# A two-block transformer kernel on one core: small vectors from one load, another order at the start, another split of the layer norms

## The chip, the cores and the metric

The kernel runs on one core of a Trainium2 chip. The metric is device time in microseconds (us), lower is better. Engines are called by their short names: PE (TensorE, matmul), DVE (VectorE), ACT (ScalarE), POOL (GpSimd), SP (the queue that issues the large loads).

## The reference, cut to what matters

256 tokens of width 1024 pass through two blocks. All is float32.

```
# first block: two layers
shift, scale, gate = split(silu(c) @ mod_w[i] + mod_b[i], 3)
h = rms_norm(x, norm_g[i]) * (1 + scale) + shift
x = x + gate * mixer_i(h)              # i = 0 retention, i = 1 forgetting attention
x = rms_norm(x, final_g)
# second block: two layers
x = layer_norm(ALPHA * x + mix_i(x), ln_mix_g[i], ln_mix_b[i])   # gated conv of 31 taps; short conv
x = layer_norm(ALPHA * x + ffn_i(x), ln_ffn_g[i], ln_ffn_b[i])   # dense SwiGLU of 2816; 8 experts, top 2
# layer_norm(z) = (z - mean) * rsqrt(var + 1e-5) * g + b
```

## The kernel before, in words

Each engine has its own program, written out by hand; semaphores tie them. An engine runs its instructions strictly in the order of its program, so that an instruction behind one that waits is late as well.

**Weights.** SP loads weights in chunks of 2 MB into a ring of three slots (`load`, L616), in the order of `LOADS`. A chunk before the experts is 512 columns of a first matrix, or 4 blocks of 128 rows of a second one. Before the chunks of weights, and between them in the retention, come halves of the three parts of `mod_w` (SCALE, SHIFT, GATE), two to a part. A slot is loaded anew when DVE has used what lay in it. A chunk is split into high and low parts for exact products, half by half (a half is a "unit"; four unit buffers): ACT copies the high part (`highs_until`, L1134), DVE subtracts (`lows_until`, L1461). ACT may write a unit buffer only when PE is done with the unit that lay there four units before (`released`, L557). Each product on PE is three matmuls (`product`, L690: lines 692 to 694).

**The start.** ACT issues the small loads: the vector `c` (8 rows), the identity and the rope exponents, the positions, eight loads of vectors, one vector to a partition, 43 rows of 1024 in all (the 31 taps of the convolution are one of them, L1105), and the rest of the constants. PE turns `c` and the vectors into columns (L797, L801) and DVE copies the columns to `vec` (L1596). DVE computes the rope angles (`angles`), multiplies and adds the rows of the SCALE and SHIFT halves of `mod_w` with silu(c) (`modulation`, L1529 and L1531; eight instructions a part), normalises x between the first and the second half (`normalise`, L1567), and PE sums over partitions (`mod_sum`, L792). SP loads x behind the first half of SCALE. When both sums are there, ACT makes the affine step on the turned x (`affine`, L1168) in four groups, DVE splits each group, and then ACT and DVE split the first two chunks of weights (`highs_until(1)`, L1187, and `lows_until(1)`, L1605). The first product waits for the whole first chunk.

**Second matrices.** `out_product` (L743) computes 2 token halves x 2 column halves in four PSUM banks. It goes through the blocks of rows with all four banks, but the last blocks (the "tail": the last 4, for `ffn_down` with its 22 blocks the last 2) first for token half 0 and then for token half 1, so that the banks of half 0 are full earlier. When a unit of the tail has been used for token half 1, it is released.

**The residual and the norms.** After `ret_out` and `fox_out`, `gated_residual` (L1587, L1589) takes bank after bank. After `conf_out`, `ffn_down` and `sc_out`, `layer_norm` (L1849) does, on DVE and for one token half after the other: z = ALPHA * x + bank and `bn_stats` for each column half (L1857, L1860), `bn_aggr`, a request to POOL for the power of -0.5 (`ask_root`, L1485; POOL's line is L1424), (z - mean) * g (L1867), a wait for the root, and x = z * root + b (L1869). Then PE transposes x (L704), ACT copies the high part out of the banks (`high_in`, L1177; for the router L1350), DVE takes the low part (`low_in`), and the next first matrix starts. Before `layer_norm` in DVE's program stands a `lows_until` for the first chunk of the next matrix; the second chunk's stands behind `low_in`.

**The experts.** Eight experts, each with 21 chunks of weights, follow in loops, and a last layer norm.

## Time and profile before

| | us |
|---|---|
| median of 3 runs (lowest to highest) | 1935.29 (1934.23 to 1935.48) |
| the profiled execution, its own time | 1935.74 |
| its span, first to last instruction | 1934.0 |
| PE busy in it | 1803.0 (93%) |
| DVE busy | 1471.2 (76%) |
| ACT busy | 1062.2 (55%) |
| POOL busy | 34.1 (2%) |

The profiled execution's time and its span differ by what lies before the first and after the last instruction. PE's busy share is an average over stages: it has gaps at the start, around the norms and where the router runs. What an edit is worth is read at the place where it stands, in the chain of waits and in the timeline of the engines there. A row of the timeline gives the start, the duration, the engine, the line, the operation and its tile, how many it merges, and in square brackets how long the engine had been idle and what released it. Busy times of neighbouring instructions on one engine overlap a little; the distance of their starts is what one costs in a row of them.

### The profile page before, as it was taken

The numbers are of one execution on the slowest core, as the hardware profiler recorded it, in microseconds if no ns is written. First come the engines' busy times: TensorE is split into PE (matmuls) and PEld (weight loads), VectorE is DVE, ScalarE is ACT, GpSimd is POOL, SyncE is SP. The second block draws the span as 40 slices with busy tenths as digits, with TensorE's granted clock in tenths as the row PEclk, the third lists the DMA queues.
The fourth block names the chain that finished last, engine by engine and source line by source line (L and its number), as shares of the span: only waits on it lengthen the run. The fifth ranks groups of instructions, "written<-read, shape, count | busy, mean of one in ns | idle before, by whom it ended". The sixth has DMA issues, their size and how long they took to land.

```text
span 1934.0 us, 23674 instructions
## 1 busy us (share of the span) xinstructions
PE 1803.0 (93%) x9475; PEld 1547.6 (80%) x9475; DVE 1471.2 (76%) x1339; ACT 1062.2 (55%) x912; POOL 34.1 (2%) x34
## 2 busy tenths in 40 slices
PE   2899889988988999897999999999999999999995
PEld 2888678868978998796788887888878888888884
DVE  5686856485976554576788888889888898888895
ACT  1334234553843333232767777767677677777772
POOL 0000002000000000000000000000000000000000
PEclk9999889999999999897999999999999999999998
DMA  9588354405304547454699999999999999999992
GB/s 339 189 301 318 114 214 162 174 14 188 138 1 137 190 153 261 142 186 152 245 339 351 368 366 337 342 354 377 350 342 346 365 361 346 354 361 371 355 380 96
DMA packets 209604, 506.75 MB, mean 262 GB/s; under 512 B 6549, under 2 KB 8877, under 8 KB 209496
## 3 DMA queue, kind: packets, MB, share of 16 engines
q1 hardware_dynamic: 204832, 498.09, 70.6%
q10 hardware_dynamic: 4488, 6.58, 1.0%
q8 instruction: 81, 1.33, 0.3%
q0 software_dynamic: 176, 0.53, 0.1%
q14 instruction: 27, 0.22, 0.0%
HBM read 504.13 MB, written 1.05 MB: 261 GB/s over the span
## 4 chain that ended last, share of the span: by engine, by line
PE 86%; DVE 8%; ACT 2%; issue 2%; DMA 1%; POOL 1%; ACTq 0%; POOLq 0%; DVEq 0%
PE psum L692 27%; PE psum L694 26%; PE psum L693 26%; DVE R L1800 2%; PE psum L1013 2%; PE psum L1041 1%; DVE units L1457 1%; DMA ring<-in_mod_w 1%; POOL root_out L1424 1%; PE psum L1082 1%; DVE stats L1860 1%; DMA R<-in_positions 0%; DVE R L1531 0%; DVE x L1869 0%; PE psum L704 0%
## 5 line engine op out<-in xcount | busy, mean ns | idle before, releaser
L1457 DVE TENSOR_TENSOR units<-ring,units 128x2048 fp32r<-128x2048 f32 x451 | 1012.5, 2278 | 241.0 <-ACT units L1148 167.9
L1365 ACT CAST units<-ring 128x2048 fp32r<-128x2048 f32 x332 | 629.7, 1914 | 244.5 <-PE psum L694 145.9
L692 PE MATMUL psum<-units,xr 128*128 128x512 f32 x1120 | 444.1, 397 | 8.0 <-issue 4.5
L694 PE MATMUL psum<-units,xr 128*128 128x512 f32 x1120 | 438.4, 391 | 0.0
L693 PE MATMUL psum<-units,xr 128*128 128x512 f32 x1120 | 438.1, 391 | 0.0
L1148 ACT CAST units<-ring 128x2048 fp32r<-128x2048 f32 (+1 forms) x119 | 218.4, 1879 | 223.2 <-PE psum L694 187.2
L692 PE MATMUL psum<-units,H 128*128 128x512 f32 x696 | 274.6, 395 | 2.2 <-DVE H L1457 2.2
L694 PE MATMUL psum<-units,H 128*128 128x512 f32 x696 | 272.4, 391 | 0.0
L693 PE MATMUL psum<-units,H 128*128 128x512 f32 x696 | 272.4, 391 | 0.0
L692 PE MATMUL psum<-xr,units 128*128 128x256 f32 x864 | 247.1, 286 | 12.7 <-DVE units L1457 11.4
L692 PEld LDWEIGHTS psum<-units,xr 128*128 128x128 f32 x1120 | 211.6, 189 | 52.7 <-issue 7.6
L694 PEld LDWEIGHTS psum<-units,xr 128*128 128x128 f32 x1120 | 211.6, 189 | 45.0
L693 PEld LDWEIGHTS psum<-units,xr 128*128 128x128 f32 x1120 | 211.8, 189 | 43.6 <-issue 0.7
L693 PE MATMUL psum<-xr,units 128*128 128x256 f32 x864 | 246.4, 285 | 0.0
L694 PE MATMUL psum<-xr,units 128*128 128x256 f32 x864 | 246.3, 285 | 0.0
L692 PEld LDWEIGHTS psum<-xr,units 128*128 128x128 f32 x864 | 168.0, 194 | 13.8 <-DVE units L1457 11.4
L693 PEld LDWEIGHTS psum<-xr,units 128*128 128x128 f32 x864 | 168.0, 194 | 0.0
L694 PEld LDWEIGHTS psum<-xr,units 128*128 128x128 f32 x864 | 167.8, 194 | 0.0
L692 PEld LDWEIGHTS psum<-units,H 128*128 128x128 f32 x696 | 131.7, 189 | 30.1 <-issue 1.9
L694 PEld LDWEIGHTS psum<-units,H 128*128 128x128 f32 x696 | 131.6, 189 | 27.7
L693 PEld LDWEIGHTS psum<-units,H 128*128 128x128 f32 x696 | 131.8, 189 | 27.0
L2014 DVE TENSOR_TENSOR R<-R,psum 128x512 f32<-128x512 f32 x56 | 38.5, 687 | 46.1 <-PE psum L694 45.8
(242 smaller groups left out, 1210.0 us busy)
## 6 DMA issues: line engine op xcount, KB each, us to landing
ring<-in_moe_w_gate SPq DMA_DIRECT2D x56, 2048.0 KB, 9.5
ring<-in_moe_w_up SPq DMA_DIRECT2D x56, 2048.0 KB, 9.4
ring<-in_moe_w_down SPq DMA_DIRECT2D x56, 2048.0 KB, 9.6
ring<-in_mod_w SPq DMA_DIRECT2D x12, 2048.0 KB, 9.9
ring<-in_ret_w_in SPq DMA_DIRECT2D x11, 2048.0 KB, 10.1
ring<-in_fox_w_in SPq DMA_DIRECT2D x8, 2048.0 KB, 8.5
ring<-in_sc_w_in SPq DMA_DIRECT2D x6, 2048.0 KB, 7.9
ring<-in_ffn_w_gate SPq DMA_DIRECT2D x5, 2048.0 KB, 8.0
```

The costliest lines, as they stand in the source:

```text
L692: mm(dst, left[0], right[0], start=first, stop=False)
L693: mm(dst, left[0], right[1], start=False, stop=False)
L694: return mm(dst, left[1], right[0], start=False, stop=last)
L1013: last = mm(psum[:, k // 4, (k % 4) * P:(k % 4 + 1) * P], x[:, tt, k * P:(k + 1) * P], e_sel[q][:, tt, :], start=(tt == 0), stop=(tt == NT ...
L1041: last = nc.tensor.transpose(b[:, j * P:(j + 1) * P], e_ht[:, (q * PAIRS + c) % 2, j * P:(j + 1) * P], ident)
L1082: last = mm(psum[:, 2 * tt + c, :], e_selT[:, tt * P:(tt + 1) * P], e_y[part][:, c * 512:(c + 1) * 512], start=(part == 0), stop=(part == 1))
L1148: nc.scalar.copy(dst[0], src).then_inc(unit_high, 3 - len(parts))
L1365: nc.scalar.copy(*expert_unit_parts(q, j, half, 0)).then_inc(unit_high, 1)
L1424: nc.gpsimd.tensor_tensor(root_out[:, n % 2, 0:w], root_in[:, n % 2, 0:w], neg_half[:, 0:w], ALU.pow).then_inc(root_ready, 1)
L1457: return v.tensor_tensor(dst, src, high.bitcast(F32), ALU.subtract)
L1800: ins = v.scalar_tensor_tensor(conv[:, i, :], u_pad[:, i, k:k + T], vec[:, i, V_DW + k:V_DW + k + 1], conv[:, i, :], ALU.mult, ALU.add)
L2014: v.tensor_tensor(e_ht[:, (q * PAIRS + c) % 2, :], e_s[:, (q * PAIRS + c) % 2, :], psum[:, 4 + (q * 2 * PAIRS + 2 * c + 1) % 4, :], ALU.mu ...
```

## The change

**Small vectors.** The host lays all vectors out feature-major, as one array of 128 partitions x 8 x 49 (three rows more than before: the shifts of three layer norms), and one load on ACT's queue, behind the constants, brings them straight to `vec`. The vector `c` comes as eight columns of the first piece of the constants. The nine small loads, PE's transposes of them and DVE's copy are gone.

**The start.** SP issues the second half of SCALE before x. DVE does both halves of SCALE before `normalise`. The first chunk of weights is split before the affine step: on ACT `highs_until(0)` stands ahead of `affine`, on DVE `lows_until(0)` stands between the second half of SHIFT and `take_sum(0, SHIFT)`. PE sums SCALE before it transposes x.

**Second matrices.** The tail goes through its blocks for token half 0, then for token half 1 and column half 0, then for token half 1 and column half 1. For `ffn_down` it is the last 6 blocks instead of the last 2. A unit of the tail is released in the third pass.

**Three layer norms** (`mix0`, `ffn0`, `mix1`). DVE does the statistics as before and (z - mean) * g in two halves of 512 columns; ACT multiplies them by the root, in place; PE transposes z, without the shift. The shift is a bias per feature, on ACT when it takes the high part (an instruction of 256 columns for each of eight blocks, before one of 512 for two blocks), and on DVE when it takes the low part (the same). Behind that DVE adds the shift to z for the x of the next residual (`shift_rows`). The last layer norm stays as it is.

```diff
...
                 sp.dma_start(dst, src).then_inc(slot_filled[at % RING], 16)
             load(0)
+            load(1)
             sp.dma_start(x[:, :, :], t["x"][0].rearrange("(t p) d -> p t d", p=P)).then_inc(x_loaded, 16)
-            load(1)
-            load(2)
-            for at in range(3, LOADED):
+            for at in range(2, LOADED):
                 load(at)
             def expert(e, q, more, number):
...
                 banks = [take_bank(OUT_BANKS[name], i) for i in range(4)]
-                def block(k, tt, w):
-                    for c in range(2):
+                def block(k, tt, w, cs=(0, 1)):
+                    for c in cs:
                         last = product(banks[2 * tt + c], [a[:, k, tt * P:(tt + 1) * P] for a in src],
                                        [a[:, k % 2, c * 512:(c + 1) * 512] for a in w], k == 0, k == blocks - 1)
                         if k == blocks - 1:
                 def weights(k):
                     return unit(CHUNK_AT[name, k // ROWS], k % ROWS // 2, lambda a: as_rows(a, 2))
-                tail = blocks % ROWS or ROWS
+                tail = blocks % ROWS + ROWS if blocks % ROWS else ROWS
                 for k in range(blocks - tail):
                     if k % 2 == 0:
                         ready(k // 2)
                         last.then_inc(weights_used, 1)
                 w = {}
-                for tt in range(NT):
+                for tt, cs in ((0, (0, 1)), (1, (0,)), (1, (1,))):
                     for k in range(blocks - tail, blocks):
                         if tt == 0 and k % 2 == 0:
                             ready(k // 2)
                             w[k // 2] = weights(k)
-                        last = block(k, tt, w[k // 2])
-                        if tt == NT - 1 and k % 2 == 1 and k < blocks - 1:
+                        last = block(k, tt, w[k // 2], cs)
+                        if cs == (1,) and k % 2 == 1 and k < blocks - 1:
                             last.then_inc(weights_used, 1)
+            def transpose_scaled(name, z, n):
+                banks = [take_bank(name, g) for g in range(4)]
+                for tt in range(NT):
+                    for g in range(4):
+                        if g % 2 == 0:
+                            pe.wait_ge(scaled, 4 * n + 2 * tt + g // 2 + 1)
+                        for j in range(2):
+                            last = nc.tensor.transpose(banks[g][:, j * T + tt * P:j * T + (tt + 1) * P],
+                                                       z[:, tt, (2 * g + j) * P:(2 * g + j + 1) * P], ident)
+                        if tt == NT - 1:
+                            last.then_inc(bank_filled, 1)
...
-            pe.wait_ge(ident_loaded, 16)
-            pe.wait_ge(c_loaded, 16)
-            nc.tensor.transpose(take_bank("c_cols", 0)[:, 0:KB], c_rows, ident[0:KB, 0:KB]).then_inc(bank_filled, 1)
-            pe.wait_ge(vec_loaded, 8 * 16)
-            b = take_bank("vecs", 0)
-            for k in range(KB):
-                last = nc.tensor.transpose(b[:, k * NVEC:(k + 1) * NVEC], vec_rows[:, k * P:(k + 1) * P],
-                                           ident[0:NVEC, 0:NVEC])
-            last.then_inc(bank_filled, 1)
-            transpose_in("x0T", xn, lambda tt: pe.wait_ge(xn_ready, tt + 1))
             pe.wait_ge(const_loaded, 16)
             mod_sum(0, SCALE)
+            pe.wait_ge(ident_loaded, 16)
+            transpose_in("x0T", xn, lambda tt: pe.wait_ge(xn_ready, tt + 1))
             mod_sum(0, SHIFT)
...
             out_product("conf_out", conf_uT, KB, lambda g: pe.wait_ge(conf_low, g + 1))
-            transpose_in("x3T", x, lambda tt: pe.wait_ge(x_ready, NT + tt + 1))
+            transpose_scaled("x3T", z_mix0, 0)
...
         @block.scalar
         def _(act):
-            act.dma_start(c_rows, t["c"].rearrange("o (k p) -> (o k) p", p=P)).then_inc(c_loaded, 16)
-            act.dma_start(const[:, 0:C_INV + 1], t["const"][:, 0:C_INV + 1]).then_inc(ident_loaded, 16)
+            act.dma_start(const[:, 0:C_TRI], t["const"][:, 0:C_TRI]).then_inc(ident_loaded, 16)
             act.dma_start(pos_i, t["positions"][0:1, :].to_broadcast([P, T])).then_inc(pos_loaded, 16)
-            for lo, src in ((V_NORM, t["norm_g"]), (V_CB, t["conf_b_dw_2"]),
-                            (V_CG, t["conf_ln_g_2"]), (V_CBETA, t["conf_ln_b_2"]),
-                            (V_SC, t["sc_w_conv_2"][0]), (V_DW, t["conf_w_dw_2"][0])):
-                act.dma_start(vec_rows[lo:lo + src.shape[0], :], src).then_inc(vec_loaded, 16)
-            for layer in range(2):
-                act.dma_start(vec_rows[V_MB + 2 * layer:V_MB + 2 * layer + 2, :],
-                              t["mod_b"][layer:layer + 1, 0:2 * D].rearrange("o (j d) -> (o j) d", d=D)).then_inc(vec_loaded, 16)
             act.dma_start(const[:, C_TRI:C_END], t["const"][:, C_TRI:C_END]).then_inc(const_loaded, 16)
+            act.dma_start(vec[:, :, :].rearrange("p k n -> p (k n)"), t["vecs"]).then_inc(vec_loaded, 16)
             def load_small():
                 act.dma_start(wf[:, :, :], cols(w_fox, 4 * D, FH)).then_inc(small_loaded, 16)
             def wait_mod_columns(i):
                 act.wait_ge(mod_columns, i + 1)
+            def scale_rows(name, z, n):
+                for tt in range(NT):
+                    i = ROOTS.index(f"{name}_{tt}")
+                    act.wait_ge(root_ready, i + 1)
+                    for half in range(2):
+                        part = z[:, tt, half * 512:(half + 1) * 512]
+                        act.wait_ge(centred, 4 * n + 2 * tt + half + 1)
+                        nc.scalar.activation(part, part, ACT.Identity, scale=root_out[:, i % 2, 0:1]).then_inc(scaled, 1)
+            def shifted_high(name, dst, n):
+                for g in range(4):
+                    b = pairs(bank(name, g))
+                    for j in range(2):
+                        k = 2 * g + j
+                        last = nc.scalar.activation(dst[:, k, :], b[:, j, :], ACT.Identity, bias=vec[:, k, V_LB + n:V_LB + n + 1])
+                    last.then_inc(bank_high, 1)
             def high_in(name, dst, n=4):
                 for g in range(n):
                     nc.scalar.copy(dst[:, 2 * g:2 * g + 2, :], pairs(bank(name, g))).then_inc(bank_high, 1)
-            nc.scalar.activation(c_act[:, :], bank("c_cols", 0)[:, 0:KB], ACT.Silu).then_inc(emptied["A"], 1)
+            act.wait_ge(ident_loaded, 16)
+            nc.scalar.activation(c_act[:, :], const[:, C_C:C_C + KB], ACT.Silu).then_inc(c_ready, 1)
             act.wait_ge(x_loaded, 16)
             square_rows(xn)
             act.wait_ge(ang_ready, 1)
             nc.scalar.activation(cos, ang[:, 4, :], ACT.Sin)
             nc.scalar.activation(sin, ang[:, 3, :], ACT.Sin).then_inc(trig_ready, 1)
+            highs_until(0)
...
-            act.wait_ge(x_ready, NT * 2)
-            high_in("x3T", xr[:, 0])
+            scale_rows("mix0", z_mix0, 0)
...
+            scale_rows("ffn0", z_ffn0, 1)
+            shifted_high("x4T", xr[:, 0], 1)
+            highs_until(CHUNK_AT["ffn_down", 5] + 2)
             act.wait_ge(x_ready, NT * 3)
             load_rows(t["ln_mix_g_2"][1:2, :], t["ln_mix_b_2"][1:2, :])
-            high_in("x4T", xr[:, 0])
...
             highs_until(CHUNK_AT["sc_out", 1] + 1)
-            act.wait_ge(x_ready, NT * 4)
+            scale_rows("mix1", z_mix1, 2)
             for g in range(4):
-                nc.scalar.copy(x5T[:, 2 * g:2 * g + 2, :], pairs(bank("x5T", g))).then_inc(emptied["A"], 1)
+                b = pairs(bank("x5T", g))
+                for j in range(2):
+                    k = 2 * g + j
+                    last = nc.scalar.activation(x5T[:, k, :], b[:, j, :], ACT.Identity, bias=vec[:, k, V_LB + 2:V_LB + 3])
...
                     v.tensor_tensor(xi, xi, y_tmp[:, i % 2, :], ALU.add).then_inc(emptied["D"], 1)
             angles()
-            dve.wait_ge(emptied["A"], 1)
+            dve.wait_ge(c_ready, 1)
             modulation(0, SCALE, 0)
+            modulation(0, SCALE, 1)
             normalise("rms0", 0, xn)
-            modulation(0, SCALE, 1)
-            v.tensor_copy(vec[:, :, :].rearrange("p k n -> p (k n)"), bank("vecs", 0)[:, 0:KB * NVEC]
-                          ).then_inc(emptied["D"], 1)
-            wait_emptied("vecs", 0)
             modulation(0, SHIFT, 0)
+            dve.wait_ge(vec_loaded, 16)
+            take_sum(0, SCALE)
             modulation(0, SHIFT, 1)
-            take_sum(0, SCALE)
+            lows_until(0)
             take_sum(0, SHIFT)
             input_affine(0)
...
             lows_until(CHUNK_AT["conf_out", 1] + 1)
-            def layer_norm(name, n, y, z, g_row=rows_gb[:, 0, :], b_row=rows_gb[:, 1, :]):
+            def statistics(name, y, z, tt):
+                for half in range(2):
+                    hs = slice(half * 512, (half + 1) * 512)
+                    if y is not None:
+                        src, count = y(tt, half)
+                        v.scalar_tensor_tensor(z[:, tt, hs], x[:, tt, hs], ALPHA, src, ALU.mult, ALU.add
+                                               ).then_inc(emptied["D"], 1)
+                        dve.wait_ge(emptied["D"], count)
+                    last = v.bn_stats(stats[:, tt, half, :], z[:, tt, hs])
+                step(last)
+                step(v.bn_aggr(meanvar[:, tt, :], stats[:, tt, :, :].rearrange("p a b -> p (a b)")))
+                ask_root(f"{name}_{tt}", meanvar[:, tt, 1:2], 1.0, LN_EPS)
+            def normed(name, n, y, z):
                 for tt in range(NT):
+                    statistics(name, y, z, tt)
+                    if tt == 0:
+                        dve.wait_ge(rows_loaded, 32 * n)
                     for half in range(2):
                         hs = slice(half * 512, (half + 1) * 512)
-                        if y is not None:
-                            src, count = y(tt, half)
-                            v.scalar_tensor_tensor(z[:, tt, hs], x[:, tt, hs], ALPHA, src, ALU.mult, ALU.add
-                                                   ).then_inc(emptied["D"], 1)
-                            dve.wait_ge(emptied["D"], count)
-                        last = v.bn_stats(stats[:, tt, half, :], z[:, tt, hs])
-                    step(last)
-                    step(v.bn_aggr(meanvar[:, tt, :], stats[:, tt, :, :].rearrange("p a b -> p (a b)")))
-                    ask_root(f"{name}_{tt}", meanvar[:, tt, 1:2], 1.0, LN_EPS)
+                        v.scalar_tensor_tensor(z[:, tt, hs], z[:, tt, hs], meanvar[:, tt, 0:1], row_g[:, hs],
+                                               ALU.subtract, ALU.mult).then_inc(centred, 1)
+            def shifted_low(name, dst, n):
+                for g in range(4):
+                    dve.wait_ge(bank_high, high_count(BANK_AT[name, g]))
+                    b = pairs(bank(name, g))
+                    for j in range(2):
+                        k = 2 * g + j
+                        last = v.scalar_tensor_tensor(dst[1][:, k, :], b[:, j, :], vec[:, k, V_LB + n:V_LB + n + 1],
+                                                      dst[0][:, k, :].bitcast(F32), ALU.add, ALU.subtract)
+                    last.then_inc(emptied["D"], 1)
+            def shift_rows(n, z):
+                for tt in range(NT):
+                    dve.wait_ge(scaled, 4 * (n - 1) + 2 * tt + 2)
+                    v.tensor_tensor(x[:, tt, :], z[:, tt, :], row_b, ALU.add).then_inc(x_ready, 1)
+                dve.wait_ge(x_ready, NT * (n + 1))
+            def layer_norm(name, n, z, g_row, b_row):
+                for tt in range(NT):
+                    statistics(name, None, z, tt)
                     if tt == 0:
                         dve.wait_ge(rows_loaded, 32 * n)
...
-            layer_norm("mix0", 1, from_banks("conf_y"), region(8448, NT, D))
-            low_in("x3T", xr_parts)
+            normed("mix0", 1, from_banks("conf_y"), z_mix0)
+            shifted_low("x3T", xr_parts, 0)
+            shift_rows(1, z_mix0)
             lows_until(CHUNK_AT["conf_out", 1] + 2)
...
```

## Rows read from the trace of the kernel before

**Rows 1.** The page: busy time, share of the span, instructions by engine
```profile
PE 1803.0 (93%) x9475; PEld 1547.6 (80%) x9475; DVE 1471.2 (76%) x1339; ACT 1062.2 (55%) x912; POOL 34.1 (2%) x34
```
**Rows 2.** The chain that ended last, the start: start us, us, what
```profile
1.80 9.10 DMA R<-in_positions
...
15.33 0.76 DVE R L1529
...
20.07 15.46 DMA ring<-in_mod_w
...
40.92 3.58 PE psum L792 x16
...
51.28 4.51 DVE units L1457 x2
```
**Rows 3.** The timeline, all engines, 22 to 56 us
```profile
22.46 0.75 DVE L1567 TENSOR_SCALAR R<-x,root_out 128x1024 f32<-128x1024 f32 x1 [0.67 <-POOL root_out L1424]
24.58 0.93 PEld L801 LDWEIGHTS psum<-const,R 43*128 43x128 f32 x8 [15.12 <-DMA R<-in_mod_b]
...
24.75 5.25 DVE L1531 SCALAR_TENSOR_TENSOR R<-ring,c_act,R 128x1024 f32<-128x1024 f32 x4 [1.54 <-DMA ring<-in_mod_w]
...
45.08 1.93 ACT L1168 ACTIVATE R<-psum,in_shift,in_scale 128x256 f32<-128x256 f32 x4 [27.92 <-DVE in_scale L1572]
...
46.59 0.69 DVE L1457 TENSOR_TENSOR xr<-R,xr 128x512 fp32r<-128x512 f32 x1
...
55.88 0.55 PE L692 MATMUL psum<-xr,units 128*128 128x256 f32 x1 [11.39 <-DVE units L1457]
```
**Rows 4.** DMA issues, 0 to 70 us: times, KB each, us to landing
```profile
R<-in_conf_w_dw ACTq DMA_DIRECT2D x1, 124.0 KB
```
**Rows 5.** Windows of 1 us, the last two columns DMA share and GB/s
```profile
27.00:28.00 1.00, 1.00 (x7) 1.00 (x6) 0.96 (x2) 0.00 (x0) 0.00 (x0) 1.00 1.02 406
...
30.00:31.00 1.00, 0.85 (x5) 0.89 (x5) 0.91 (x2) 0.00 (x0) 0.00 (x0) 1.00 0.06 25
```
**Rows 6.** The timeline after `ret_out`, DVE
```profile
269.38 0.69 DVE L1587 TENSOR_TENSOR R<-psum,gate 128x512 f32<-128x512 f32 x1 [2.69 <-PE psum L694]
...
270.71 0.68 DVE L1587 TENSOR_TENSOR R<-psum,gate 128x512 f32<-128x512 f32 x1
```
**Rows 7.** The timeline after `conf_out` (norm mix0)
```profile
583.74 1.28 DVE L1867 SCALAR_TENSOR_TENSOR R<-R,meanvar 128x1024 f32<-128x1024 f32 x1
583.90 1.52 POOL L1424 TENSOR_TENSOR root_out<-root_in,neg_half 128x1 f32<-128x1 f32 x1 [25.78 <-DVE root_in L1485]
...
586.73 0.68 DVE L1857 SCALAR_TENSOR_TENSOR R<-x,psum 128x512 f32<-128x512 f32 x1
...
591.60 1.29 DVE L1869 SCALAR_TENSOR_TENSOR x<-R,root_out 128x1024 f32<-128x1024 f32 x1 [0.52 <-POOL root_out L1424]
...
593.73 2.05 ACT L1177 CAST xr<-psum 128x512 fp32r<-128x512 f32 x4 [15.87 <-PE psum L704]
594.40 2.48 DVE L1457 TENSOR_TENSOR xr<-psum,xr 128x512 fp32r<-128x512 f32 x4 [1.51 <-ACT xr L1177]
595.24 0.55 PE L692 MATMUL psum<-xr,units 128*128 128x256 f32 x1 [0.32 <-DVE xr L1457]
```
**Rows 8.** The timeline after `ffn_down` (norm ffn0)
```profile
772.18 1.91 ACT L1148 CAST units<-ring 128x2048 fp32r<-128x2048 f32 x1 [8.95 <-PE psum L694]
777.62 1.91 ACT L1148 CAST units<-ring 128x2048 fp32r<-128x2048 f32 x1 [3.53 <-PE psum L694]
...
781.77 0.68 DVE L1857 SCALAR_TENSOR_TENSOR R<-x,psum 128x512 f32<-128x512 f32 x1
...
796.40 0.55 PE L692 MATMUL psum<-xr,units 128*128 128x256 f32 x1 [0.38 <-DVE xr L1457]
```
**Rows 9.** The timeline before the router
```profile
895.53 2.05 ACT L1350 COPY R<-psum 128x512 f32<-128x512 f32 x4 [15.86 <-PE psum L704]
...
897.63 7.00 PE L986 MATMUL psum<-w_router,R 128*128 128x8 f32 x32 [0.92 <-ACT R L1350]
```

56 lines of the change are left out of this document (37 added, 19 removed).

## The prediction

> **What bounds the kernel now.** The page comes first: PE is busy for 93% of the span [rows 1], so time can only be won where PE stands still. The chain of waits says where. At the start it runs over the positions' load, then over DVE's sums of `mod_w` from 15.33 to 40.9 us, PE's sum over partitions, and the split of the first chunk [rows 2]; PE's first product begins at 55.88 us, released by DVE's split [rows 3]. After that PE is the chain, with short breaks behind each second matrix [rows 6 to 9]. So I read the timeline of each engine at the start and at these breaks, and the DMA's windows at the start.
>
> Durations are of the profiled execution (1935.74 us), which lies 0.45 us above the median of the runs; the sum is made against it, and 0.45 is taken off at the end.
>
> **The start.** DVE is the bound from the landing of the positions. Their issue moves up by about 0.6 us, since one load instead of two stands ahead of it: they land at 10.3 instead of 1.80 + 9.10 = 10.9 [rows 2]. From there DVE needs what it needs now:
> - angles 15.33 - 10.9 = 4.4, to 14.7;
> - first half of SCALE 20.07 - 15.33 = 4.74, to 19.45 [rows 2];
> - second half 5.28, to 24.7. Now it waits 1.54 us for its load, until 24.75 [rows 3];
> - `normalise`, with POOL's two roots, 22.46 + 0.75 - 20.07 = 3.14, to 27.9. Now it stands between the two halves, and DVE idles only for the 1.54 us that are left until the load is there;
> - first half of SHIFT 4.74, and the small sum 0.2, to 32.8; second half 5.28, to 38.1. The present one ends at 40.92;
> - the low parts of the first chunk 4.51 [rows 2], to 42.6. PE's sum over partitions, 3.58, runs beside it and costs nothing; without that cover it would add its 3.6;
> - small columns 0.5, affine from 43.1. Its first group is split 46.59 + 0.69 - 45.08 = 2.2 us later [rows 3], and PE starts at 45.3.
>
> 55.88 - 45.3 = **10.6 us** won. ACT splits the first chunk (1.91 a unit [rows 8]) while DVE is at SHIFT, and hides. The second chunk's split ends near 56 us, inside PE's 96 matmuls of the first, which I put at 11 us or more: their mean in the run is 0.19 [rows 1]. If that cover went, the loss would be under 1 us. The other groups of the affine step come 1.2 us apart; if PE outruns them it loses up to 0.7, if its clock rises earlier than now it wins up to 1.5.
>
> This holds if the loads come in time, and now they do not: PE gets the last small vector only at 24.58, and the second half of SCALE comes at 24.75 [rows 3]. In the windows the core moves 406 GB/s up to 28 us, but at 30 to 31 us the share is 0.06, which is one engine of 16, while the second half of SHIFT (20.07 + 15.46 = 35.5) has not landed [rows 2, 5]. So one DMA engine is some 6 us behind, and all wait for it. The 31 taps are one load of 124 KB [rows 4]; on a single engine (406 / 16 = 25 GB/s) that is 5.0 us, and the other vectors add about 1. One load from 128 partitions leaves the engines even. Then the loads of 2 MB, 5.2 us each, end near 16.5 (second SCALE), 19 (x), 24 (SHIFT) and 29.5 us, always before DVE comes to them, and the first chunk near 35. I take this; the other end is the first rival.
>
> The Trainium skill, DMA: Bandwidth & Descriptors, section "Why a DMA increments its semaphore by 16 and not by 1", says that a load uses the largest number of engines up to 16 that divides its outer dimension, the lowest-numbered ones: 31 rows go to one engine, 128 partitions to all 16. The trace's one late engine agrees. By a rule of even spreading of rows the lag would have another cause and stay, which is the first rival's case.
>
> **The residuals after `ret_out` and `fox_out`.** Bank 2 is now full a pass of 12 matmuls before the end. Two blocks of rows are 24 matmuls and take 777.62 - 772.18 = 5.44 us [rows 8], so 12 take 2.72. DVE idles for 2.69 us just there [rows 6]. One bank's two instructions cost 270.71 - 269.38 = 1.33 (two of 0.69, overlapping) [rows 6]; they move in front of the end: 2 x 1.33 = **2.7 us** won.
>
> **The norm after `conf_out`.** Now from DVE's first instruction on token half 1 to PE's first product: 595.24 - 586.73 = 8.51 [rows 7]. After the change, the same stretch: statistics and centring 591.60 - 0.52 - 586.73 = 4.35, less 1.33 for the column half that is now done before PE ends; the root 0.4 behind the centring (583.90 + 1.52 against 583.74 + 1.28); ACT's first half 0.1 + 0.58; transposes 593.73 - 592.89 = 0.84; ACT's two instructions of 256 columns 1.05 (four take 1.93 [rows 3]) where one of 512 took 0.6; DVE's two 0.9 where one took 0.7. Sum 6.9, so 593.6: **1.5 us** won. DVE's price for 256 columns out of PSUM with a bias is not shown; half and the whole of the present 0.62 bound it, and the range of the gain is 1 to 2. The first group alone counts, as PE's first matmuls are slower than the groups' pace. Behind it `shift_rows` (two of about 1.3, as the instruction it replaces) stands before the second chunk's split; both hide under PE's first chunk, with about 3 us to spare, and would cost up to 2.6 if they did not.
>
> The root's 1.52 is POOL standing still while DVE centres. The Trainium skill, SBUF — State Buffer, section "SBUF: two separate sides", calls the port pair of DVE and POOL an exclusive lock for a whole instruction. With two short instructions in place of one, POOL could get in between them: by that rule each norm wins or loses some 0.5 us more, by the row as I use it nothing.
>
> **The norm before the router.** The same up to ACT's reading, which then starts 2.05 us earlier than 895.53, but takes eight instructions, 3.8 us, where four took 2.05; PE waits for all: 897.35 against 897.63 [rows 9]: **0.3 us** won, between -0.5 and 1.
>
> **The norm after `ffn_down`.** Here the tail turns against the change. DVE's program has the split of the first chunk of `sc_c` in front of the norm; its two units need the buffers of blocks 16 to 19. Now these are free at 772.18 and 777.62, and the norm starts at 781.77 [rows 8]. PE ends at 777.6 + 5.44 = 783.1. With a tail of 6 they are released in the third pass, which starts 18 matmuls (4.1 us) before the end, at 779.0: after 6 and 12 matmuls, at 780.4 and 781.7. ACT 1.91, DVE 2.29 and 2.25 behind it: 786.8. So the norm starts 5.0 us later, and nothing of it lies ahead of PE's end any more. Then token half 0 takes 4.35 instead of 6.07 (no wait for the root, no last product) and token half 1 takes 6.9 + 1.33 = 8.2: PE starts at 799.4 instead of 796.40: **3.0 us** lost. PE's order and SP's loads hold no further stall: the ring's later slots come free 5 us later, against 11 us of products before the data are due.
>
> **The sum.** 10.6 + 2.7 + 1.5 + 0.3 - 3.0 = 12.1 us. 1935.74 - 12.1 - 0.45 = **1923.2 us**. The last layer norm and the experts are untouched and move along.
>
> **Rivals.**
> - *The late engine stays.* For it: the lag's cause is inferred, and instruction and software queues use the engines too. Then second SCALE lands at 24.75 less the 2.6 us of x, which stands behind it now, so 22.1; it ends at 27.4, `normalise` at 30.5, first SHIFT at 35.4; second SHIFT lands at 35.5 as now and ends at 40.9. The low parts end at 45.4 and PE starts at 48.2: 7.7 won instead of 10.6, time 1926.1.
> - *The `ffn_down` stall is not there*, because ACT's and DVE's splits find room I do not see. Then that norm wins 1.5 as after `conf_out`: 1918.7. Against it: both programs are in order.
> - *The late release bites behind all five second matrices.* It would decide if a split in front of the residual or norm needed a unit of the tail. Each norm then loses 3.0, each residual 6.2 (DVE starts 3.7 after PE's end and has four banks of 1.33, against 2.7 now): 10.6 - 9.0 - 12.4 = -10.8, time 1946. Against it: with 8 or 16 blocks the units needed are of the chunk before the tail.
>
> **How the numbers follow.** Forecast 0.52, late engine 0.23, no stall 0.11, all tails 0.04; 0.10 is left for a start that wins under half for a reason not seen. The range 1918.5 to 1929 holds the first three with 2.5 us above the second. Under 0.2% (3.9 us) this kernel's timing can't tell from no change: faster 0.88, same 0.07, slower 0.05.
>
> **What would show it.** PE's first product near 45 us with DVE without a gap from 10.3 (near 48 with a wait of DVE near 20: the late engine); DMA share without the hole at 29 to 31 us; bank 2 taken before PE's end; after `ffn_down`, DVE's last split ending some 3.7 us after PE's last product. Wrong would be: PE's start after 50, or a wait of PE for units in the retention.

## The result

| | before | after |
|---|---|---|
| time, us (median of 4 runs each) | 1935.38 (1934.23 to 1941.57) | 1915.30 (1914.73 to 1917.3) |
| ratio, 95% interval | | 0.9898 (0.9881 to 0.9915) |
| profiled execution: time, span, granted clock | 1935.74, 1934.0, 0.974 | 1915.32, 1913.5, 0.974 |
| PE's first product | 55.88 | 44.49 |

The change makes the kernel 20.1 us faster. The forecast was 12.1 us less, 1923.2, with a range of 1918.5 to 1929: the direction is right, the time lies below the range.

The page of the kernel after, the line that answers to [rows 1]:

```profile
PE 1794.5 (94%) x9466; PEld 1542.0 (81%) x9466; DVE 1472.9 (77%) x1352; ACT 1074.7 (56%) x936; POOL 30.9 (2%) x34
```

PE is busy for 8.5 us less, and has only nine small matmuls fewer. So part of the 20 us is not shorter waits, but the same matmuls done in less time. Every span below is read from one profiled execution of a kernel.

**The start**, timeline of the kernel after [rows 2, 3]:

```profile
9.74 0.29 DVE L1536 CAST R<-R 128x256 f32<-128x256 int32 x1 [9.74 <-DMA R<-in_positions]
...
14.92 9.21 DVE L1571 SCALAR_TENSOR_TENSOR R<-ring,c_act,R 128x1024 f32<-128x1024 f32 x7
...
32.04 5.25 DVE L1571 SCALAR_TENSOR_TENSOR R<-ring,c_act,R 128x1024 f32<-128x1024 f32 x4
...
37.21 4.48 DVE L1497 TENSOR_TENSOR units<-ring,units 128x2048 fp32r<-128x2048 f32 x2
...
44.49 0.55 PE L707 MATMUL psum<-xr,units 128*128 128x256 f32 x1 [3.58 <-DVE xr L1497]
```

From 9.74 on DVE waits for no load any more, and the chunk's split (L1497 at 37.21) lies ahead of the affine step. In its windows (the last two columns are DMA share and GB/s) the hole of [rows 5] is gone:

```profile
27.00:28.00 1.00, 1.00 (x6) 1.00 (x7) 0.96 (x3) 0.00 (x0) 0.00 (x0) 1.00 1.01 401
...
30.00:31.00 1.00, 1.00 (x7) 0.88 (x5) 0.96 (x2) 0.00 (x0) 0.00 (x0) 1.00 1.06 389
```

**Behind `ret_out`**, DVE after [rows 6]. The third bank is taken before PE's end, and the fourth is left:

```profile
254.38 0.69 DVE L1627 TENSOR_TENSOR R<-psum,gate 128x512 f32<-128x512 f32 x1 [0.65 <-PE psum L709]
...
257.10 0.69 DVE L1627 TENSOR_TENSOR R<-psum,gate 128x512 f32<-128x512 f32 x1 [1.30 <-PE psum L709]
```

Only half of a bank's price is won here. In the kernel before DVE took the third bank at 269.38 [rows 6], 0.64 us ahead of PE's end at 270.02, and was through with the fourth 2.10 us behind that end; now it is through 1.45 us behind it. PE's break from its last product to its next one goes from 8.54 to 7.90 us, and behind `fox_out` from 8.55 to 7.90.

**The norm behind `conf_out`** after [rows 7]:

```profile
571.87 1.40 DVE L1911 SCALAR_TENSOR_TENSOR R<-R,meanvar 128x512 f32<-128x512 f32 x2
572.03 0.99 POOL L1464 TENSOR_TENSOR root_out<-root_in,neg_half 128x1 f32<-128x1 f32 x1 [3.82 <-DVE root_in L1525]
573.05 1.33 ACT L1195 ACTIVATE R<-R,root_out 128x512 f32<-128x512 f32 x2 [3.47 <-POOL root_out L1464]
573.82 1.97 PE L802 MATMUL psum<-const,R 128*128 128x128 f32 x8 [2.88 <-ACT R L1195]
574.55 3.03 ACT L1203 ACTIVATE xr<-psum,vec 128x256 fp32r<-128x256 f32 x8 [0.17 <-PE psum L802]
...
576.44 0.55 PE L707 MATMUL psum<-xr,units 128*128 128x256 f32 x1 [0.65 <-DVE xr L1921]
```

POOL's root ends 1.15 us after DVE began to centre, where it ended 1.68 after in the kernel before [rows 7].

**The norm behind `ffn_down`** after [rows 8]:

```profile
762.33 3.71 ACT L1160 CAST units<-ring 128x2048 fp32r<-128x2048 f32 x2 [17.11 <-PE psum L709]
...
764.27 4.49 DVE L1497 TENSOR_TENSOR units<-ring,units 128x2048 fp32r<-128x2048 f32 x2 [16.65 <-ACT units L1160]
764.56 0.39 PE L709 MATMUL psum<-units,H 128*128 128x512 f32 x1
...
768.68 0.68 DVE L1894 SCALAR_TENSOR_TENSOR R<-x,psum 128x512 f32<-128x512 f32 x1
...
773.80 1.94 PE L802 MATMUL psum<-const,R 128*128 128x128 f32 x8 [8.85 <-DVE R L1894]
...
780.72 0.55 PE L707 MATMUL psum<-xr,units 128*128 128x256 f32 x1 [0.65 <-DVE xr L1921]
```

PE ends its last product at 764.95. DVE begins to split the two units of the next matrix only at 764.27 and is at it until 768.76, so that the norm starts 3.7 us behind PE's end; PE's next product comes 15.77 us after its last, where it came after 13.43. **Ahead of the router** [rows 9] the break of PE went from 9.09 to 7.57:

```profile
881.35 6.99 PE L1005 MATMUL psum<-w_router,R 128*128 128x8 f32 x32 [1.84 <-ACT R L1389]
```

**Stages without an edit.** Windows of the same work, first before and then after: the stretch, its length, busy time and count on PE, PEld, DVE, ACT and POOL, PE's granted clock, DMA share, GB/s. They are the retention from the first product to its first statistics, fox from its first product to its last, the first expert, and the expert pair with the loop's first return.

```profile
55.88:210.24 154.36, 154.36 (x855) 133.41 (x856) 111.78 (x113) 53.09 (x42) 1.40 (x2) 1.00 0.71 263
278.56:449.86 171.30, 162.45 (x896) 135.54 (x896) 108.92 (x209) 80.96 (x136) 13.13 (x8) 0.97 0.35 125
920.39:973.63 53.24, 51.96 (x244) 43.51 (x245) 41.66 (x26) 37.50 (x26) 0.00 (x0) 0.97 0.74 271
1097.14:1223.96 126.82, 124.87 (x574) 103.50 (x573) 108.50 (x64) 91.53 (x60) 0.00 (x0) 0.99 0.96 352
```

```profile
44.49:197.89 153.40, 153.40 (x855) 132.46 (x856) 115.03 (x119) 57.91 (x47) 1.41 (x2) 0.99 0.74 270
264.96:432.86 167.90, 159.06 (x896) 133.35 (x896) 109.59 (x210) 81.03 (x136) 13.14 (x8) 0.99 0.36 127
903.75:955.47 51.72, 50.44 (x244) 42.38 (x245) 41.64 (x26) 37.51 (x26) 0.00 (x0) 1.00 0.77 278
1078.80:1203.78 124.98, 123.37 (x575) 102.48 (x574) 108.55 (x64) 91.64 (x60) 0.00 (x0) 1.00 0.98 357
```

The same 244 matmuls of the first expert take 1.5 us less busy time at a granted clock of 1.00 than at 0.97 (2.4 GHz all through, against a part at 1.2). The loop's return shows the same. The retention doesn't: it is 0.96 shorter at 0.99 than at 1.00. In fox, the same 896 matmuls take 3.4 us less, and most of it comes from one place. Behind the same break of PE, 1.90 us in both kernels, the kernel before runs 6.83 us at half the clock and the changed kernel, in the same work, does not:

```profile
423.21:430.04 6.83, 6.11 (x21) 4.25 (x20) 5.00 (x8) 4.08 (x3) 0.00 (x0) 0.50 0.01 2
```

```profile
408.98:415.81 6.83, 6.12 (x33) 4.82 (x32) 5.83 (x8) 4.10 (x3) 0.00 (x0) 1.00 0.01 2
```

A shorter break can also cost clock. Behind `conf_out` the granted clock is at half for 6.83 us in both kernels, and it starts 3.7 us (before) and 3.4 us (after) behind PE's last product. What is left of it when the products begin is 2.05 us before and 3.85 us after:

```profile
595.24:597.29 2.05, 2.05 (x9) 2.05 (x10) 1.64 (x3) 2.05 (x3) 0.00 (x0) 0.50 0.00 0
```

```profile
576.44:580.29 3.85, 3.85 (x18) 3.85 (x19) 3.85 (x8) 3.85 (x6) 0.00 (x0) 0.50 0.00 0
```

By an estimate from these two rows, 1.8 us more at half the pace cost 0.9 us; the `ffn` stage is 0.78 longer.

**The account**, spans in us; a break runs from the end of PE's last product to its next product, or to the router's:

| stretch | predicted | won |
|---|---|---|
| start, to PE's first product | 10.6 | 11.39 |
| breaks behind `ret_out` (8.54 to 7.90), `fox_out` (8.55 to 7.90) | 2.7 | 1.3 |
| break behind `conf_out` (8.50 to 6.37) | 1.5 | 2.13 |
| break ahead of the router (9.09 to 7.57) | 0.3 | 1.52 |
| break behind `ffn_down` (13.43 to 15.77) | -3.0 | -2.34 |
| *edited stretches together* | *12.1* | *14.0* |
| retention with `ret_out` 1.57, fox 3.39 | 0 | 5.0 |
| products of `conf_out` -0.97, `ffn` -0.78, `sc` -0.93 | 0 | -2.7 |
| router to first gather 0.36, experts 3.78 | 0 | 4.1 |
| all | 12.1 | 20.4 |

### The profile page after: what moved, and what is told of

It is laid out like the page before. It is cut to its first block, busy times and chain, and to the rows that moved or that the text cites. A ratio compares the mean times of both kernels' runs of the same rounds, so it can differ in the third digit from the quotient of the medians.

```text
span 1913.5 us, 23684 instructions
## 1 busy us (share of the span) xinstructions
PE 1794.5 (94%) x9466; PEld 1542.0 (81%) x9466; DVE 1472.9 (77%) x1352; ACT 1074.7 (56%) x936; POOL 30.9 (2%) x34
## 3 DMA queue, kind: packets, MB, share of 16 engines
q8 instruction: 81, 1.33, 0.3%
## 4 chain that ended last, share of the span: by engine, by line
PE 88%; DVE 8%; ACT 2%; issue 2%; POOL 0%; DMA 0%; ACTq 0%; POOLq 0%; DVEq 0%
PE psum L707 27%; PE psum L709 27%; PE psum L708 27%; DVE R L1839 2%; PE psum L1032 2%; PE psum L1060 1%; DVE R L1571 1%; DVE units L1497 1%; PE psum L1101 1%; POOL root_out L1464 0%; DMA R<-in_positions 0%; PE psum L1005 0%; PE psum L925 0%; DVE stats L1897 0%; PE psum L944 0%
## 5 line engine op out<-in xcount | busy, mean ns | idle before, releaser
L1497 DVE TENSOR_TENSOR units<-ring,units 128x2048 fp32r<-128x2048 f32 x451 | 1013.2, 2278 | 230.1 <-ACT units L1160 164.8
## 6 DMA issues: line engine op xcount, KB each, us to landing
ring<-in_mod_w SPq DMA_DIRECT2D x12, 2048.0 KB, 10.6
ring<-in_ret_w_in SPq DMA_DIRECT2D x11, 2048.0 KB, 10.1
```

What stands on the lines that cost most here:

```text
L1497: return v.tensor_tensor(dst, src, high.bitcast(F32), ALU.subtract)
```

## The experiments

Each ran beside the kernel before. None leaves work of the computation out. Differences are between medians; those against the changed kernel (1915.30, run beside 1935.38) would be up to 1.6 us larger if taken by the ratios, as the kernel before showed 1933.79 to 1934.56 beside the others.

**1. The start taken apart.** `row_load_back` gives one load of 31 rows back; `split_late` splits the first chunk behind the wait for the small vectors, as before; `x_first` swaps two loads; `one_load_only` is the kernel before with only the small vectors in one load.

```
row_load_back
+ act.dma_start(R[0:TAPS, 8192:8192 + D], t["conf_w_dw_2"][0]).then_inc(taps_loaded, 16)
...
+ act.wait_ge(taps_loaded, 16)        # behind highs_until(1), ahead of load_small()
split_late
- highs_until(0)                      # ACT, ahead of the wait for vec
- lows_until(0)                       # DVE, ahead of take_sum(0, SHIFT)
x_first
- load(0); load(1); x    + load(0); x; load(1)
one_load_only (in the kernel before)
- (eight loads of rows, PE's transposes of them, DVE's copy)
+ act.dma_start(vec[:, :, :].rearrange("p k n -> p (k n)"), t["vecs"]).then_inc(vec_loaded, 16)
```

> The changed kernel with one load added on ACT's queue in front of the rest of the constants: the 31 taps, one to a partition, into scratch (its result is not used). Theory: 31 partitions go over one DMA engine (124 KB), which falls 5 us behind, and every load of SP waits for it: DVE waits some 2.5 us for the second half of SCALE and again for the second half of SHIFT, PE's first product comes at 47.5 to 48.5 instead of 44.5, the total near 1918.5 (+-3). Rival (the lag had another cause: queues of instructions or of software): the first product stays at 44.5.

> The changed kernel with the first chunk split behind the affine step again, on ACT and DVE. Theory: DVE's 4.5 us no longer lie beside PE's sum over partitions, and ACT's 3.7 us stand between the affine step and DVE's split: affine starts near 41.5 instead of 42.1, its groups end near 47, the second unit's low part near 52.3, PE's first product at 52.3 instead of 44.5: 7.8 us slower, near 1923 (+-3 for the clock). Rival (the early split only moves work that was hidden): the first product within 2 us of 44.5.

> The changed kernel with x loaded in front of the second half of SCALE, as before. Theory: with even DMA engines the second half lands near 19 us in either order, DVE comes to it at 19.4, and the order is worth nothing: first product at 44.5 (+-0.5), total 1915.3 (+-3). Rival: DVE waits up to 2.6 us for it, first product up to 47.

> The kernel before with one edit: the vectors come feature-major in one load from 128 partitions behind the constants, without PE's transposes and DVE's copy; order of DVE, loads and splits as before. Theory: no DMA engine falls behind, DVE's 1.54 us wait for the second half of SCALE and its copy of 0.5 us go, the second half of SHIFT ends near 38.5 instead of 40.9, first product near 53.4 instead of 55.9: 2.5 us faster than the kernel before (+-3 for the clock). Rival (the lag stays): the wait for the second half of SCALE stays, first product at 55.4.

Measured: first product 48.37, 51.83, 45.23 and 53.33; times 1922.14 (ratio 0.9934, 0.9917 to 0.9951), 1925.43 (0.9951, 0.9936 to 0.9966), 1920.77 (0.9926, 0.9909 to 0.9943) and 1932.54 (0.9992, 0.9983 to 1.0002). In `row_load_back` DVE gets its wait back:

```profile
22.42 5.25 DVE L1574 SCALAR_TENSOR_TENSOR R<-ring,c_act,R 128x1024 f32<-128x1024 f32 x4 [3.80 <-DMA ring<-in_mod_w]
```

So one load of 124 KB from 31 rows is enough to hold DVE up for 3.8 us; the rule of the Trainium skill on the number of engines (DMA: Bandwidth & Descriptors, section "Why a DMA increments its semaphore by 16 and not by 1") agrees with it. The load alone gives 2.6 us of the start (55.88 to 53.33), the early split 7.3 (51.83 to 44.49), and 1.5 are left, of which the order of SP's two loads gives 0.7 (`x_first`, 45.23 to 44.49) and the rest is not taken apart. The first products came out as expected, within 0.5 us (for `x_first` 0.2 outside the bounds given). Of the four times, `split_late` and `one_load_only` lie within the 3 us allowed, `row_load_back` and `x_first` do not. Against the changed kernel the first three are +6.8, +10.1 and +5.5, with +3.9, +7.3 and +0.7 in the start. The other 2.8 to 4.7 us are lost in stages that are the same code.

**2. The tail of `ffn_down` and the column order.**

```
tail_as_before
- tail = blocks % ROWS + ROWS if blocks % ROWS else ROWS
+ tail = blocks % ROWS or ROWS
tail_of_four
+ tail = ROWS
- lows_until(first); normed("ffn0", ...)
+ lows_until(first - 1); low_half(first, 0); normed("ffn0", ...); low_half(first, 1)
columns_together
- for tt, cs in ((0, (0, 1)), (1, (0,)), (1, (1,))):
+ for tt, cs in ((0, (0, 1)), (1, (0, 1))):      # units of the tail released in this pass
```

> The changed kernel, but the tail of ffn_down is the last 2 blocks again, as before the change (the order of token and column halves stays new). Theory: the tail of 6 makes DVE's split wait for units that are released in the third pass; with 2 blocks DVE's norm starts some 1.3 us before PE's last product instead of 3.7 us behind it, and the stretch from PE's last product of ffn_down to the next first product falls from 15.8 to about 11 us: 4.6 us faster, near 1910.7 (+-3 for the clock). Rival: the longer tail pays, since the banks of token half 0 are full 4 us earlier; then this kernel is slower than the changed one.

> The changed kernel with a tail of the last 4 blocks for ffn_down, and on DVE the low part of the first half chunk of sc_c in front of the norm, that of the second half behind its centring. Theory: only the second unit now waits for the tail; its split falls into DVE's idle time while ACT scales, so the stretch from ffn_down's last product to the next first product falls from 15.8 to about 6.5 us as after conf_out: 9 us faster than the changed kernel, near 1906 (+-3). Rival (the stretch is bound by ACT and POOL, not by the split): 1911 or more.

> The changed kernel, but the tail's token half 1 again takes both column halves block by block. Theory: the residuals after ret_out and fox_out lose 1.33 us each, the norms after conf_out and sc_out 1.3 each, while after ffn_down the units are released earlier and DVE's norm starts about 2.3 us behind PE's last product instead of 3.7: in sum 3.9 us slower, near 1919 (+-3); in the profile each of these stages moves by its own amount. Rival (the early third bank is worth nothing, since DVE is busy): no stage but ffn_down's moves.

Measured: PE's break behind `ffn_down` 10.85, 6.38 and 13.57; times 1916.47 (0.9903, 0.9886 to 0.9919), **1908.30** (0.9863, 0.9847 to 0.9880) and 1917.90 (0.9907, 0.9890 to 0.9923). `tail_of_four`:

```profile
758.76 0.69 DVE L1900 SCALAR_TENSOR_TENSOR R<-x,psum 128x512 f32<-128x512 f32 x1 [0.47 <-PE psum L709]
...
771.23 0.55 PE L707 MATMUL psum<-xr,units 128*128 128x256 f32 x1 [0.65 <-DVE xr L1927]
```

The norm starts 9.9 us earlier than in the changed kernel, on the first full bank, and PE's break is 6.38 as behind `conf_out`. The stall is what the prediction said, the late release of the units by a longer tail, and avoiding it is worth 9.4 us in the break and 7 us in the time: this version beats both kernels. `tail_as_before` won its 4.9 in the break and lost it again, among other places where the granted clock is low in the first expert (53.30 against 51.72) and at the loop's return (127.36 against 124.98); its time is 2.8 us above what was allowed.

`columns_together` gives the column order its price, in the changed kernel: PE's break is 8.54 against 7.90 behind `ret_out`, 8.55 against 7.90 behind `fox_out`, 7.01 against 6.38 behind `conf_out` and 8.19 against 7.57 ahead of the router. That is 0.6 us at each of the four, where 1.3 were expected; behind `ffn_down` the old order wins 2.2. Its time says less: its four executions were 1914.05 and 1916.54 at mean granted clocks of 0.979 and 0.978, and 1919.26 and 1920.84 at 0.971 and 0.970.

**3. The layer norms alone** (names of the functions in place of the code).

```
norms_as_before
- transpose_scaled / scale_rows / shifted_high / normed / shifted_low / shift_rows
+ transpose_in / high_in / layer_norm / low_in          (as in the kernel before)
norms_shifted (the same, and)
+ for i in range(14): step(v.memset(pad[:, i:i + 1], 0.0))   # ahead of DVE's first wait
```

> The changed kernel with the three layer norms as before the change (DVE multiplies by the root and adds the shift before PE transposes); start, tail and order of its halves stay new. Theory: the stretch from PE's last product of conf_out to the next first product grows from 6.38 to 7.2 us, after ffn_down from 15.8 to 18.4, and before the router by about 0.3: 3.7 us slower, near 1919 (+-3). Rival (ACT's doubled instructions eat what DVE saves): the stretches stay within 0.5 us of the changed kernel's.

> The kernel with the layer norms as before (1939.3), in which VectorE issues 14 memsets of one column each before its first wait, where it is idle until 9.4 us, so that its expert loop stands 14 instructions further on in its program, where it stands in the changed kernel. In the kernel without them VectorE stood still for 7.7 and 8.0 us at the loop's two returns and waited for nothing that the profile shows, and the stages of these two returns were 5.5 and 5.7 us longer than in the changed kernel. Theory (the stall hangs on where the loop stands in VectorE's program): both stalls are gone, 1927 to 1930. Rival (it hangs on what else moves at that time, such as the weight loads): they stay, 1938 to 1940.

Measured: 1939.30 (1.0022, 1.0012 to 1.0032) and 1926.55 (0.9959, 0.9946 to 0.9971). The break behind `ffn_down` was as expected, 18.30. Behind `conf_out` it was 8.49 where 7.2 was expected, and ahead of the router 9.09: with the old norms the new column order is worth nothing there (8.50 and 9.09 in the kernel before), since DVE comes to the third bank only when PE has ended. Of the 20 us that were not expected, 17 lay in the experts. At the loop's first return, DVE of `norms_as_before`, then of `norms_shifted`:

```profile
1165.79 2.48 DVE L2107 SCALAR_TENSOR_TENSOR R<-psum,gate_of,R 128x1024 f32<-128x1024 f32 x2
1175.93 4.49 DVE L1493 TENSOR_TENSOR units<-ring,units 128x2048 fp32r<-128x2048 f32 x2 [7.66 <-issue]
```

```profile
1167.17 2.48 DVE L2110 SCALAR_TENSOR_TENSOR R<-psum,gate_of,R 128x1024 f32<-128x1024 f32 x2
1169.56 4.49 DVE L1493 TENSOR_TENSOR units<-ring,units 128x2048 fp32r<-128x2048 f32 x2
```

DVE stands still for 7.66 us on nothing that the profile shows, and for 7.96 at the second return. Fourteen idle memsets, which put its loop 14 instructions further on, take both stalls away and 12.8 us off the time. The kernels were profiled once each; that the ten times of `norms_as_before` (1936.4 to 1940.5) and the six of `norms_shifted` (1923.8 to 1927.3) lie apart says that the stall is no matter of one execution. The Trainium skill, Runtime: NRT & Kernel Launch, section "Instruction fetch mechanics", says that a taken branch whose target isn't among the two blocks of instructions held must wait for a fetch; the pair of runs agrees. But `one_load_only` has its loop after the same number of DVE instructions as `norms_as_before` and shows no stall, so the place by count isn't the whole rule. What else decides is open. Without this stall the new norms are worth 1926.55 - 1915.30 = 11.3 us, of which the edited stretches hold 6.2: 8.50 - 6.38 = 2.12 behind `conf_out`, 18.30 - 15.77 = 2.53 behind `ffn_down`, and 9.09 - 7.57 = 1.52 ahead of the router.

**4. Is it the granted clock?** Two kinds of test. Pauses put DVE to idle work ahead of the second half of SHIFT, and so move everything behind it, in either kernel:

```
delay1_*, delay3_*
+ step(v.memset(pad, 0.0))
+ for _ in range(1):          # 3 in delay3_*
+     step(v.tensor_scalar(pad, pad, 1.0, None, ALU.mult))
```

> The changed kernel with a pause of DVE (one memset and one product over 1024 columns of scratch, estimated 1.6 us) before the second half of SHIFT; nothing else differs. The changed kernel beat the forecast by 8 us, and 5.2 us of its gain lie in stages that no edit touches, where the granted clock comes back earlier. Theory 'clock': after a break of PE the low clock lasts longer or shorter by where the break falls in time, so a pure shift changes those stages by parts of a us to 2 us each: the total is off 1915.3 + pause by over 1 us, either way. Rival 'steady': the edits themselves make these stages shorter; then the total is 1915.3 + 1.6 = 1916.9 within 0.5, and every later stage is as long as in the changed kernel.

> The same with three products, estimated 3.2 us. Clock: off 1918.5 by over 1 us, and by another amount than with the short pause. Steady: 1918.5 within 0.5.

> The kernel before with the pause of about 1.6 us at the same place. Clock: off 1935.3 + 1.6 = 1936.9 by over 1 us; it may even be faster than the kernel before. Steady: 1936.9 within 0.5.

> The kernel before with the pause of about 3.2 us. Clock: off 1938.5 by over 1 us. Steady: 1938.5 within 0.5.

Fillers give PE work in its breaks, with the same waits:

```
busy_breaks, four_busy (on tail_of_four), in transpose_scaled
+ for _ in range(((0, 10), (33, 9), (0, 10))[n][tt]):     # ((0, 10), (4, 4), (0, 10)) in four_busy
+     nc.tensor.transpose(banks[0][:, tt * P:(tt + 1) * P], ident, ident)
```

> The changed kernel with TensorE given work in three of its breaks: transposes of the identity into a bank that the next instructions overwrite anyway, 10 before the second block's transposes of the norm behind conf_out, 33 before the first and 9 before the second behind ffn_down, 10 before the second ahead of the router. No value that the kernel returns changes, and each group fits into the idle time that the changed kernel has there (2.88, 8.85, 2.36 and 2.89 us at 0.24 each). Theory (what the sum left out is the granted clock after breaks of TensorE): the first products behind conf_out (4.4 us) and behind ffn_down (5.1 us) no longer run at a granted clock of about a half, which gives 2.2 and 2.5 us: 1910 to 1911.5, with the stage from the first product behind ffn_down to mix1's last bank near 90.5 instead of 93.1. Rival (the pace after a break is set by VectorE's and ScalarE's splits, the clock only goes along): 1914.5 to 1916.5. Rival (filler of this kind does not keep the clock): the granted clock of those stretches stays at a half, and the time with it.

> The kernel with ffn_down's tail of four rows (1908.3), with the same kind of filler: 10 identity transposes in the norm behind conf_out, 4 and 4 behind ffn_down, 10 ahead of the router. By the granted clock: 2.2 us behind conf_out and up to 2.0 behind ffn_down, 1904 to 1906. By the rivals: 1907.5 to 1909.5.

Measured (us against the base's median; for the kernel before 1933.79, run beside them):

| run | first product later | time | beyond the pause |
|---|---|---|---|
| delay1_after | 1.56 | 1921.14, +5.8 | 4.3 |
| delay3_after | 3.03 | 1923.15, +7.9 | 4.8 |
| delay1_before | 1.96 | 1935.87, +2.1 | 0.1 |
| delay3_before | 2.94 | 1938.00, +4.2 | 1.3 |
| busy_breaks | -0.22 | 1920.79, +5.5 | |
| four_busy (against 1908.30) | -0.19 | 1907.82, -0.5 | |

In the changed kernel a pause of 1.56 us costs 5.8: its four executions lie at 1919.5 to 1922.4, all of them above the slowest of the changed kernel, 1917.3, by more than the pause. So moving this kernel in time costs it 4 us and more. In the kernel before the pauses cost little more than themselves, 0.1 and 1.3 us beyond. The median of `delay3_before` lies within the half us of the rival 'steady' (1938.5); that of `delay1_before` is 1.0 below its figure, but the kernel before was itself 1.5 below the 1935.3 from which that figure was made. For that kernel the times don't bear the theory out.

The stages show where time can move. Fox with its residual is the clearest; the first two of these three kernels don't differ in it by an instruction. The kernel before, `delay3_before`, and the changed kernel:

```profile
272.12:451.96 179.84, 166.10 (x912) 138.84 (x912) 113.84 (x220) 84.09 (x142) 15.15 (x11) 0.95 0.35 123
```

```profile
275.24:451.69 176.45, 162.36 (x912) 136.44 (x912) 113.86 (x219) 84.11 (x142) 15.15 (x11) 0.98 0.35 126
```

```profile
258.51:434.31 175.80, 162.32 (x912) 136.43 (x912) 113.88 (x220) 84.17 (x142) 15.17 (x11) 0.98 0.36 126
```

The very same 912 matmuls take 3.7 us less busy time in the second row than in the first, which is clock (0.98 against 0.95). That the pause did it isn't shown. The profiled execution of `delay3_before` took 1935.42 at a mean granted clock of 0.977, and of its eight executions only one other was like it; six took 1936.7 to 1940.1 at 0.966 to 0.974. The kernel before, profiled in an execution of 1935.74 at 0.974, does the same without any pause: of 53 executions beside these runs, nine took 1931.9 to 1932.9 at 0.977, and 33 were at 0.963 to 0.969, with a median of 1934.1. At 0.977 the two kernels lie 2.9 us apart, which is the pause. So executions of one kernel differ by as much as the two rows do, and one profile per kernel can't part the pause from the execution. All twelve kernels with the new column order show 175.8, of which 0.64 us less come from the shorter break behind `ret_out`; `one_load_only` and `delay1_before` show 179.7. `columns_together` lies between, 178.34 at 0.96. The first expert has two values as well, 51.7 in eight of the 17 kernels, 53.1 to 53.3 in the others.

The fillers are to change the clock on purpose. The first stretch behind `conf_out`'s and behind `ffn_down`'s norm, after and then `busy_breaks`, and behind `conf_out`'s norm in `four_busy`:

```profile
576.44:588.49 12.05, 12.05 (x86) 12.05 (x87) 8.97 (x10) 5.33 (x7) 0.00 (x0) 0.84 0.15 42
780.72:790.32 9.60, 9.60 (x64) 9.60 (x65) 8.98 (x11) 5.31 (x7) 0.00 (x0) 0.77 0.30 110
```

```profile
577.95:590.00 12.05, 12.05 (x99) 12.03 (x100) 8.96 (x10) 5.48 (x8) 0.00 (x0) 1.00 0.15 40
780.40:790.00 9.60, 9.60 (x69) 9.60 (x70) 8.99 (x11) 5.32 (x7) 0.00 (x0) 0.84 0.34 112
```

```profile
576.76:588.81 12.05, 12.05 (x88) 12.05 (x89) 8.97 (x10) 5.32 (x7) 0.00 (x0) 0.86 0.15 39
```

In `busy_breaks`, with PE busy in the break, 99 instead of 86 matmuls fit into the first 12 us, and the `ffn` stage to the first bank is 1.6 us shorter (190.66 against 192.24). So the clock does set the pace of this stretch. But the same ten fillers at the same place in `four_busy` brought 88 matmuls instead of 86 and 0.2 us of that stage. The filler doesn't keep the clock up reliably, and what decides is open. `four_busy` took 1907.82, which is what its rivals said (1907.5 to 1909.5), not the clock theory (1904 to 1906). The 1910 to 1911.5 expected of `busy_breaks` was missed by far: behind `ffn_down` only 0.6 came of 2.5, and at the loop's returns PE now stands still twice instead of once. PE there, of `busy_breaks`, after and before:

```profile
1157.99 0.49 PE L707 MATMUL psum<-units,xr 128*128 128x512 f32 x1 [2.18 <-issue]
1163.52 0.50 PE L708 MATMUL psum<-units,xr 128*128 128x512 f32 x1 [0.69 <-issue]
```

```profile
1158.81 0.49 PE L707 MATMUL psum<-units,xr 128*128 128x512 f32 x1 [1.61 <-issue]
```

```profile
1177.35 0.63 PE L692 MATMUL psum<-units,xr 128*128 128x512 f32 x1 [1.95 <-issue]
```

Those two stages are 3.3 and 2.3 us longer than in the changed kernel, which eats the gain; PE's matmuls behind the pause come 0.43 us apart there and in the kernel before, and 0.23 in the changed kernel. Of all 17 kernels only the changed kernel and `tail_of_four` pass the first return in 125.0, with PE's pause at 1.61 and 1.65; the pause is 1.87 or more in the others, and the stage 126.0 to 131.0. At the second return it is the same: the four kernels with a pause of 1.50 to 1.76 pass it in 124.3 to 124.9, all others, with 1.98 to 2.80, in 125.3 or more, the changed kernel among them (2.30, 125.65). The pause isn't a matter of PE's program alone, which is the same in `delay1_after` and the changed kernel: 2.31 and 1.54 us there, 1.61 and 2.30 here.

## Why the prediction was wrong

- **The term that was missing.** The step that failed is the one that put the stages without an edit at nothing: "The last layer norm and the experts are untouched and move along", and no term at all for the retention, fox and the products behind the norms. They gave 6.4 of the 8.3 us by which 20.4 exceeds 12.1; the edited stretches gave the other 1.9. Experiment 4 shows that these stages have more than one value for the same instructions: 3.4 us in fox, 1.5 in the first expert, 1.8 and more at the loop's return, with the granted clock going along and, in fox, one stretch at half the clock making up most of the difference. The range reached only 4.7 us below the forecast, for the ends of edited steps.
- **The start**: right in mechanism and nearly in size, 11.39 for 10.6. Positions came at 9.74 instead of 10.3 (0.6 of the 0.8). DVE had no gap. The rival of the late engine was wrong, and `row_load_back` shows that the load of 31 rows was the cause.
- **The residuals**: 1.3 for 2.7, so this term was twice too large. It took both of DVE's last banks to wait for PE's end; the third was already taken 0.64 us ahead of it, and only the rest of its 1.33 could be won. `columns_together` gives the same 0.64 for each of the two.
- **The norm behind `conf_out`**: 2.13 for 1.5 (the prediction's own terms make 1.6). Under-sized by ACT's pieces of 256 columns, which come 0.38 us apart (3.03 for eight) where I took 0.52, and by POOL's root, 1.15 after the start of centring, not 1.68. By the lock rule of the Trainium skill (SBUF — State Buffer, section "SBUF: two separate sides") POOL gets in between DVE's two short instructions; the trace agrees, as its root takes 0.99 us in place of 1.52, and the 0.5 us that the sum left out came.
- **The norm before the router**: 1.52 for 0.3. ACT's reading starts 2.50 us sooner after PE's last product, not 2.05, and its eight pieces take 3.03, not 3.8. `columns_together` puts 0.62 of the 1.52 to the column order; the other 0.9 are the new norm's.
- **The norm behind `ffn_down`**: -2.34 for -3.0, right in mechanism (`tail_of_four` removes it; `tail_as_before` takes 4.9 us off the break). The two units' splits ended 3.81 after PE's last product, as worked out (3.7), and the same half us of the norm as behind `conf_out` came on top.
- **Given back.** The products behind the breaks took longer, at the same number of matmuls: 0.78 us in `ffn`, 0.97 and 0.93 in `conf_out`'s and `sc`'s stages. For `ffn` the rows in the result show that it is clock; for the other two it isn't shown.

What stays open: which of its values a stage gets can't be told from these runs ahead of time, and they don't part what the kernel does from what one execution happens to get; each kernel has one profile. Nor do they show why the changed kernel gets the lower value in fox, the first expert and at the first return. Six variants of it (the two pauses, `x_first`, `row_load_back`, `split_late`, `tail_as_before`) lost 3 to 6 us beyond their edit, while its own four executions stayed within 2.6 us of each other. So I read 14 of the 20 us as the edits' own, and 6 as what the untouched stages happened to give, which a small further change can take away.

## What to carry to other kernels

Sum the edited stretches, then widen the range by what the untouched stages vary in granted clock: look in the trace of before for stages that run partly at the low clock behind a break, and count each as a gain or loss of 1 to 3.5 us, either sign (an estimate from the 0.8 to 3.4 us of the stages here). A load of 31 rows among large ones held up the ones behind it here; small vectors laid out over 128 partitions did not. Before you count an instruction as moved out of a wait, read how much of it lay behind the end that is waited for: here it was half. One profile doesn't tell a kernel's value of a stage from an execution's; where the times of a kernel scatter with its mean granted clock, profile it more than once. When a tail is made longer to free a bank early, check which buffers it releases late, and put the norm ahead of the split that waits for them. An experiment that misses by 10 us may have met a stall at a loop's return: look there before blaming the edit.
